# Weight sums of a seven-product block multiplication moved from VectorE to GpSimd

## The reference, cut to what matters

```python
h = rmsnorm(x, norm_ffn_g[i])
x = x + jnp.square(jax.nn.relu(h @ mlp_w1[i])) @ mlp_w2[i]
gate = jax.nn.sigmoid(x @ ple_w_gate[i])
x = x + rmsnorm(p[i] @ ple_w_proj[i], ple_norm_g[i]) * gate
```

## Time and profile before

| | |
|---|---|
| runs | 2385.16 us median of 3 (2384.28 to 2388.14) |
| profiled execution, its own time | 2383.71 us |
| its span on the core | 2381.9 us |
| TensorE busy | 2198.7 us, 92% |
| VectorE busy | 959.2 us, 40% |
| GpSimd busy | 10.3 us |
| granted TensorE clock, mean | 0.967 of full |

### The profile page before, as it was taken

One profiled execution on the slowest core, in us unless ns is written; L12 is line 12 of the kernel. 1 busy time (PEld: TensorE's weight loads), 2 busy tenths in 40 slices (PEclk: granted clock), 3 DMA queues, 4 the chain that ended last, 5 costly groups with the idle time before them and its releaser, 6 DMA issues.

```text
span 2381.9 us, 21911 instructions
## 1 busy us (share of the span) xinstructions
PE 2198.7 (92%) x9430; PEld 1356.2 (57%) x9430; DVE 959.2 (40%) x1409; ACT 369.2 (16%) x766; POOL 10.3 (0%) x22
## 2 busy tenths in 40 slices
PE   6999998999998899989996998999999987689998
PEld 5886665974485596444443544444444465348873
DVE  2654674644327464531536833112100136542210
ACT  2322110000113100020112611101000001121100
POOL 0000000000000000000000000000000000000000
PEclk9999998999999999999998998999999989799999
DMA  4225694353342244351110001111222133012432
GB/s 177 107 107 214 256 359 167 142 200 136 146 172 106 89 173 177 124 188 64 71 71 36 1 36 71 71 71 71 73 81 76 53 130 139 0 71 106 163 146 80
DMA packets 21584, 280.95 MB, mean 118 GB/s; under 512 B 2624, under 2 KB 2752, under 8 KB 4208
## 3 DMA queue, kind: packets, MB, share of 16 engines
q1 hardware_dynamic: 19712, 269.13, 30.0%
q0 software_dynamic: 1776, 10.43, 1.2%
HBM read 278.50 MB, written 1.05 MB: 117 GB/s over the span
## 4 chain that ended last, share of the span: by engine, by line
PE 84%; DVE 13%; ACT 2%; issue 1%; DMA 0%; DVEq 0%; ACTq 0%
PE bank L325 83%; DVE small L784 1%; DVE arena L670 1%; DVE HT L607 1%; DVE HT L612 1%; DVE arena L805 1%; PE bank L563 1%; DVE arena L574 0%; DVE arena L2628 0%; DVE arena L631 0%; DVE arena L950 0%; PE bank L716 0%; DMA ring<-in_W 0%; DVE arena L798 0%; ACT arena L594 0%
## 5 line engine op out<-in xcount | busy, mean ns | idle before, releaser
L325 PE MATMUL bank<-HT,ring 128*128 128x256 f32 (+2 forms) x3120 | 845.9, 433 | 18.3 <-DVE HT L612 14.4
L325 PEld LDWEIGHTS bank<-HT,ring 128*128 128x128 f32 x3120 | 559.6, 193 | 300.0 <-issue 235.6
L325 PE MATMUL bank<-ring,arena 128*128 128x512 f32 x1020 | 446.2, 598 | 10.2 <-DVE arena L1944 7.7
L325 PE MATMUL bank<-arena 128*128 128x128 f32 (+10 forms) x2784 | 420.4, 335 | 34.4 <-DVE arena L2619 8.2
L325 PEld LDWEIGHTS bank<-arena 128*128 128x128 f32 (+4 forms) x2784 | 299.2, 184 | 149.4 <-issue 91.5
L325 PEld LDWEIGHTS bank<-ring,arena 128*128 128x128 f32 x1020 | 194.6, 192 | 255.1 <-issue 242.8
L325 PE MATMUL bank<-ring,HT 128*128 128x512 f32 (+2 forms) x512 | 196.4, 543 | 7.9 <-ACT arena L572 3.1
L572 ACT ACTIVATE arena<-bank 128x512 f32<-128x512 f32 (+2 forms) x157 | 87.2, 575 | 603.5 <-PE bank L325 570.3
L325 PEld LDWEIGHTS bank<-ring,HT 128*128 128x128 f32 x512 | 91.5, 194 | 109.2 <-issue 100.2
L670 DVE RECIPROCAL arena<-arena 128x2048 f32<-128x2048 f32 (+2 forms) x8 | 87.6, 10953 | 136.4 <-ACT arena L687 136.4
L1784 DVE TENSOR_TENSOR arena<-bank,arena 128x512 f32<-128x512 f32 x24 | 16.6, 692 | 270.9 <-PE bank L325 270.8
(11 more groups left out here) (282 smaller groups left out, 1356.3 us busy)
## 6 DMA issues: line engine op xcount, KB each, us to landing
ring<-in_W SPq DMA_DIRECT2D x121, 2048.0 KB, 7.8
ring<-in_W SPq DMA_DIRECT2D x4, 1536.0 KB, 6.3
ring<-in_W SPq DMA_DIRECT2D x4, 1024.0 KB, 9.1
arena<-in_rel POOLq DMA_DIRECT2D x1, 2048.0 KB, 10.0
arena<-in_rpb POOLq DMA_DIRECT2D x1, 2048.0 KB, 8.1
arena<-in_dft POOLq DMA_DIRECT2D x2, 640.0 KB, 12.4
KC<-in_const SPq DMA_DIRECT2D x1, 1057.5 KB, 9.5
X<-in_x SPq DMA_DIRECT2D x1, 1024.0 KB, 4.9
```

The source lines that it names most:

```text
L325: return nc.tensor.matmul(out_, lhsT, rhs, start=start, stop=stop, skip_group_check=True)
```

## The change

The eight dependent groups of weight sums of each MLP (four of the up product, four of the down product, four operations each) are issued on GpSimd (`nc.gpsimd.tensor_tensor`) and count on a semaphore of their own, `sums_done`. A new function `pool_mlp` holds them in order and stands behind the loads of `pT` and the row in GpSimd's program. TensorE's waits for weight sums and SP's waits for `summed` go by `sums_done`. For the sums of activations TensorE waits on a new mark, `up{i} tokens`. The operations, their shapes and their operands stay the same.

```diff
-                        pe.wait_ge(vector_done, at(f"{label} right{n}.{j}"))
+                        pe.wait_ge(sums_done, at(f"{label} right{n}.{j}"))
...
-        def dve_right_sums(label, n, names, kt, TB):
-
-            if n >= 1:
-                dve.wait_ge(tensor_done, at(f"{label} done{n - 1}"))
+        def pool_right_sums(label, n, names, kt, TB):
+
+            adder.wait_ge(tensor_done, at(f"{label} done{n - 1}") if n else at(f"up{label[-1]} done"))
...
-            tt(T1, B12, B11, ALU.subtract).then_inc(vector_done, dve.one())
-            dve.mark(f"{label} right{n}.5")
-            tt(T3, B22, B12, ALU.subtract).then_inc(vector_done, dve.one())
-            dve.mark(f"{label} right{n}.7")
-            dve.wait_ge(vector_done, dve.n)
-            tt(T2, B22, T1, ALU.subtract).then_inc(vector_done, dve.one())
-            dve.mark(f"{label} right{n}.6", f"summed {names[1]}")
-            dve.wait_ge(vector_done, dve.n)
-            tt(T4, T2, B21, ALU.subtract).then_inc(vector_done, dve.one())
-            dve.mark(f"{label} right{n}.4", f"summed {names[0]}")
+            pool_tt(T1, B12, B11, ALU.subtract).then_inc(sums_done, adder.one())
+            adder.mark(f"{label} right{n}.5")
+            pool_tt(T3, B22, B12, ALU.subtract).then_inc(sums_done, adder.one())
+            adder.mark(f"{label} right{n}.7")
+            adder.wait_ge(sums_done, adder.n)
+            pool_tt(T2, B22, T1, ALU.subtract).then_inc(sums_done, adder.one())
+            adder.mark(f"{label} right{n}.6", f"summed {names[1]}")
+            adder.wait_ge(sums_done, adder.n)
+            pool_tt(T4, T2, B21, ALU.subtract).then_inc(sums_done, adder.one())
+            adder.mark(f"{label} right{n}.4", f"summed {names[0]}")
...
-                        pe.wait_ge(vector_done, at(f"{label} sum{q}.{j}"))
+                        pe.wait_ge(sums_done, at(f"{label} sum{q}.{j}"))
+                        pe.wait_ge(vector_done, at(f"{label[:3]} tokens"))
...
+        def pool_mlp(i):
+
+            adder.wait_ge(vector_done, at(f"ffn{i} ready 1"))
+            for p in range(4):
+                l = f"up{i}.{p}"
+                pool_row_sums(l, 0, up_pair(i, p), slice(0, 512), US, (5, 7), prev=f"up{i}.{p - 1}" if p else None)
+                pool_row_sums(l, 0, up_pair(i, p), slice(0, 512), US, (6, 3), prev=f"up{i}.{p - 1}" if p else None)
+            for n, (names, kt) in enumerate(down_chunks(i)):
+                pool_right_sums(f"down{i}", n, names, kt, M["right"])
...
             dve_token_sums(f"up{i}", HT[:, :, 0:P], HT[:, :, P:SEQ], UT)
-            dve_row_sums(f"up{i}.0", 0, up_pair(i, 0), slice(0, 512), US, (5, 7))
-            dve_row_sums(f"up{i}.0", 0, up_pair(i, 0), slice(0, 512), US, (6, 3))
+            dve.mark(f"up{i} tokens")
...
-                if p < 3:
-                    dve_row_sums(f"up{i}.{p + 1}", 0, up_pair(i, p + 1), slice(0, 512), US, (5, 7), prev=l)
                 dve_seven_c(l, 0, "w", b[:, :, 0:P], UM1, k4)
...
             dve.mark(f"hidden{i}")
-            dve.wait_ge(tensor_done, at(f"up{i} done"))
             for n, (names, kt) in enumerate(down_chunks(i)):
-                dve_right_sums(f"down{i}", n, names, kt, M["right"])
...
-                        e.wait_ge(vector_done, at("summed " + PLAN[i - RING][0]))
+                        e.wait_ge(sums_done, at("summed " + PLAN[i - RING][0]))
...
+                pool_mlp(i)
```

More of the change, by code:

```diff
@@ L223, in build @@
         tensor_done, scalar_done, vector_done = sem("tensor_done"), sem("scalar_done"), sem("vector_done")
+        sums_done = sem("sums_done")
         slot_loaded = [sem(f"slot_loaded{i}") for i in range(RING)]
@@ L226, in build @@
         loaded = {n: sem("loaded_" + n) for n in LOADS}
-        sems = {"pe": tensor_done, "act": scalar_done, "dve": vector_done, **loaded}
+        sems = {"pe": tensor_done, "act": scalar_done, "dve": vector_done, "pool": sums_done, **loaded}
         marks = {}
@@ L299, in build @@
         dve = Steps(nc.vector, vector_done, marks)
+        adder = Steps(nc.gpsimd, sums_done, marks)
+        pool_tt = nc.gpsimd.tensor_tensor
         def open_bank(name, b=None):
@@ L411, in dve_left_sums @@
             dve.mark(f"{label} left{n}")
-        def dve_right_sums(label, n, names, kt, TB):
-            if n >= 1:
-                dve.wait_ge(tensor_done, at(f"{label} done{n - 1}"))
+        def pool_right_sums(label, n, names, kt, TB):
+            adder.wait_ge(tensor_done, at(f"{label} done{n - 1}") if n else at(f"up{label[-1]} done"))
             hk = kt // 2
             for x in names:
-                dve.wait_ge(slot_loaded[WAT[x] % RING], 16 * (WAT[x] // RING + 1))
+                adder.wait_ge(slot_loaded[WAT[x] % RING], 16 * (WAT[x] // RING + 1))
             w0, w1 = (ring[:, WAT[x] % RING, 0:kt * 512].rearrange("p (k c) -> p k c", k=kt) for x in names)
@@ L501, in pe_seven_rows, with pool_row_sums @@
                     marks[f"{label} {c}{q}"] = marks[f"{label} p{q}.{j}"]
-        def dve_row_sums(label, q, names, cols, S, which, prev=None):
+        def pool_row_sums(label, q, names, cols, S, which, prev=None):
             w0, w1 = (ring[:, WAT[x] % RING, :].rearrange("p (k c) -> p k c", k=KT)[:, :, cols] for x in names)
             for x in names:
-                dve.wait_ge(slot_loaded[WAT[x] % RING], 16 * (WAT[x] // RING + 1))
+                adder.wait_ge(slot_loaded[WAT[x] % RING], 16 * (WAT[x] // RING + 1))
             hk = KT // 2
@@ L514, in dve_row_sums @@
                     if prev:
-                        dve.wait_ge(tensor_done, at(f"{prev} p{q}.{j}"))
+                        adder.wait_ge(tensor_done, at(f"{prev} p{q}.{j}"))
                     if j in (6, 3):
-                        dve.wait_ge(vector_done, dve.n)
-                    tt(d, a, b, op).then_inc(vector_done, dve.one())
-                    dve.mark(f"{label} sum{q}.{j}")
+                        adder.wait_ge(sums_done, adder.n)
+                    pool_tt(d, a, b, op).then_inc(sums_done, adder.one())
+                    adder.mark(f"{label} sum{q}.{j}")
             if which[-1] == 3:
-                dve.mark(*(f"summed {x}" for x in names))
+                adder.mark(*(f"summed {x}" for x in names))
         def dve_token_sums(label, h0, h1, T):
@@ L1937, in dve_mlp @@
                 dve.mark(f"up{i}.{p} joined")
-                if p < 3:
-                    dve_row_sums(f"up{i}.{p + 1}", 0, up_pair(i, p + 1), slice(0, 512), US, (6, 3), prev=l)
                 dve.wait_ge(vector_done, dve.n)
```

## The result

The changed kernel takes 2473.05 us (median of 4, 2471.17 to 2473.58) against 2385.18 us: a ratio of 1.0365 (95% interval 1.0347 to 1.0383), 3.7% slower. The forecast was 2471 us. The profiled execution took 2473.41 us with a span of 2471.6 us, 89.7 us more than before.

A forecast was written before the change was run, and what follows sets the result against it. TensorE, busy 92% of the span, bounds the kernel, so only its waits count. Start 2383.71 plus 86 us (43 an MLP, the middle of 48 and 38) gives 2471 us; range 2445 to 2505, or 2402 to 2505 with A (2412).

The forecast's parts named there:

- case B: Both MLPs: VectorE operations on two SBUF operands and GpSimd's sums take turns; 43 us an MLP, 2471 us; chance 0.58.
- strict alternation: Both MLPs: VectorE and GpSimd alternate operation for operation on the shared path; 48 us an MLP.
- g: Price of one weight sum of 2048 columns on GpSimd, taken as 4.6 us, twice VectorE's.
- The start, +11.2: Up product, pair 0: token sums alternate with GpSimd's first sums, ending at 427.7 where product 5 wanted them at 416.5.
- The up product, +18.4: Whole up product ends 18.4 us late, the start's 11.2 included, with fourth sums 29 us apart in place of 26.6.
- the 4 us for clock: Slower TensorE clock after each of two longer waits an MLP: some 4 us each time, left to the range.
- The last square, +18.0: Last join and squares meet down chunk 0's sums; `hidden` comes 21.9 us after the up product in place of 3.9.
- The down product, +11.5: Down product: 4.5 and 2.5 us of loads at chunks 1 and 2, 0.9 for late T4, 3.6 in last chunk.
- case C: Whole kernel not slower: GpSimd quick enough, 4.0 us a sum or less, without turns; 2389 us; chance 0.09.
- the second variant of case B: VectorE, once in, keeps the path for its whole run: up product +22.4, `hidden` +4, down product +11.4; 38 us an MLP.
- case D: GpSimd's sum far dearer than 4.6 us: +105 at 6 us, 2490 us; over 2700 at 10.95; chance 0.06.
- A (2412): Engines run beside each other, only GpSimd's slower sums cost: 13.5 us an MLP, 27 for two, 2412 us; chance 0.27.

The follow-up runs named there:

- the run with two meetings less: Changed kernel with GpSimd's first weight sum waiting for VectorE's token sums and its first down sum for the last square: 2428.08 us, ratio 1.0185.
- the run without meetings: Changed kernel with later GpSimd starts, and VectorE's squares and activation sums moved to where GpSimd waits for a load: 2420.99 us, ratio 1.0155.

## Why the prediction was right

**The mechanism, case B.** The engines take turns; every number of the forecast rests on that, and the runs with work on which nobody depends show it by itself. Which of its two variants would happen I could not tell, and took the middle, 43 us an MLP, between 48 (an operation for an operation) and 38 (VectorE keeps the path for its run). The timelines show the first: even squares that wait for nothing between them are let in one by one, 4.9 us apart. It measured 44.0 and 44.5. So the total came out within 2 us partly by luck, as the middle of two variants covered an over-priced true one: strict alternation was 4 us an MLP too dear in my sum. The signs that I had named for case B are all there: VectorE's 128x512 operations on two SBUF operands last some 4 us longer while those with a PSUM operand don't, product 5 begins at 427.44, the last square is 20.4 us behind the up product, and a pair takes over 26 us. Its terms:

- *g.* Taken 4.6; measured 4.50 where a sum meets nothing. The Trainium skill (GPSIMD Engine Reference, Elementwise — side-by-side cycle accounting) says 4497 ns, and the trace agrees. The price of a meeting was my own error: I let each add VectorE's whole 0.7 us to GpSimd, and it adds 0.3 to 0.45.
- *The start, +11.2.* Product 5 waited 9.8 us and began 15.55 us after its MLP's first product, where it had begun after 5.67: 9.9 later. The next 64 matmuls then took 10.04 us where they had taken 7.31, so another 2.7 of lost clock. That belongs to the 4 us for clock that I had left to the range.
- *The up product, +18.4.* Measured 17.8 and 17.5. The size is right for a slightly wrong reason: the pair's loop came out at 27.2 us (S4 ends at 469.31, 496.58, 523.73), not 29, which made up for the clock that the sum lacked.
- *The last square, +18.0.* Measured 16.6 in both MLPs: four meetings of some 4.2. For the clock behind the longer wait I had kept some 4 us more in the range. None of it was needed: the first 24 matmuls took 12.26 us after 20.4 us of waiting, exactly as after 3.84 (in mlp1 13.39 and 13.28).
- *The down product, +11.5.* Measured 9.55 and 10.45. The wait ahead of chunk 2 was 3.88 us for the 4.5 of the sum. The 2.5 ahead of the last chunk are absent as a wait: behind the 3.88 the granted clock was 0.86, chunk 2 took 26.1 us in place of 24.0, and the load landed meanwhile. The last chunk's waits came to 2.6 in three parts for 3.6, and it took 3.4 us longer in all. By chunks the 9.55 are 0, 4.0, 2.1 and 3.4.

The clock, for the start and the last square (window, length, TensorE, weight loads, VectorE, ACT, GpSimd busy, then granted clock):

```profile
412.00:427.00 15.00, 5.66 (x32) 5.46 (x32) 14.93 (x4) 0.60 (x1) 14.84 (x4) 0.73 0.15 62
427.00:438.00 11.00, 10.56 (x71) 10.59 (x72) 0.68 (x2) 0.60 (x1) 4.68 (x1) 0.73 0.01 1
...
532.00:552.00 20.00, 0.04 (x1) 0.00 (x0) 19.89 (x5) 0.00 (x0) 19.05 (x4) 0.59 0.28 105
552.00:564.00 12.00, 11.54 (x23) 5.12 (x24) 0.41 (x1) 0.00 (x0) 0.00 (x0) 0.84 0.15 34
```

Behind each of the two waits the granted clock lies below full for the next 11 or 12 us, at 0.73 and 0.84, as it did at 0.86 in the earlier trace rows. Not every wait is followed by that: in the run with two meetings less, 3.59 us of waiting ahead of chunk 2 in mlp0 left the clock at 1.00, and the 24 matmuls took 10.54 us.

**Slips in the sums.** Three terms of the prediction don't add up as written, and none moves the forecast. In case C, 3g + 0.1 at g = 4.0 passes 10.3 by 1.8 us, not 2.2. In the second variant of case B the up product's parts (2.9, 7.6, 7.6, 4.8) make +22.9, not +22.4. In case D, 25 us for each us of g beyond 4.6 make some +97 at 6 us, not +105.

**Edits priced at nothing.** The load of `rel` still waited 50 us for other work, so 32 sums ahead of it cost nothing. VectorE's relief gave nothing. The `tokens` wait, priced at nothing only for engines that run beside each other, is the 9.8 us of the start. The ISA instruction ahead of GpSimd's first sum, which had no row, cost nothing that TensorE saw: it stands at 407.1 us, and the first sum begins at 411.93, less than 0.1 behind the norm that it waits for. Whatever it sets off is over within those 4.8 us.

**The rivals.** A (2412) priced GpSimd alone at 27 us. The run nearest to it, with most meetings gone, costs 37.5, but a few are left in it and GpSimd starts later in it, so A's own price was not measured apart. C, a quick GpSimd, falls with g = 4.5. D, a dear one, falls too.

**Not settled.** Why the clock fell behind some waits and not behind others. 1.07 us of the loss stand ahead of mlp0, where nothing differs; I take them for a difference between two executions. Why a load in the run without meetings took 9.1 us was not tried.

## What to carry to other kernels

Work is not moved to an idle engine for free when that engine reads by a way that the busy one also uses. GpSimd's sum of two SBUF operands and VectorE's take turns by whole instructions, so a 0.69 us operation of VectorE becomes one of 4.9. Before moving, ask which VectorE operations of two SBUF operands will run beside it, and who waits for their end; the meetings that hurt are the few at whose end TensorE waits: avoiding two such places an MLP, on the same engines with the same instructions, gave back some 43 of the 88 us. And a wait for all parts of an operand, where the consumer needs the first part first, is worth splitting with or without such a change: it gave 12.6 us to the kernel before, and 37.3 (36.2 by the excess over before) to the changed one.

## What the runs showed of the hardware

- Turns between VectorE and GpSimd go one instruction for one, also when VectorE has several ready in a row (the squares L1950 to L1952 end 4.9 to 5.4 us apart); VectorE's recorded durations include the wait, 0.69 us shown as 4.87 to 5.0, so the engine looks busier with less work.
- The price is lopsided: 4.2 us for VectorE's short operation, 0.3 to 0.45 for GpSimd's long one. Against VectorE's 2.29 us sums GpSimd's last up to 6.46.
- A GpSimd copy of one operand also blocks (2.26 us for a 0.69 us operation); a fill does not (0.691), and operations of VectorE with one operand in PSUM are untouched (0.68). Squares count as two SBUF operands although both are the same tile.
- A GpSimd copy of 128 x 2048 f32 takes 1.89 us when nothing blocks it, a fill 1.80.
- A wait of 20.4 us of TensorE cost no more clock afterwards than one of 3.84: 12.26 us for the same 24 matmuls. A wait of 3.59 in another kernel cost none: 10.54.
